# Attention of a hybrid layer: values as weights and the shares of two to four heads as the moving side, shares divided before they are stored, and gates transposed early

## The reference, cut to what matters

```
q_b = rms_norm(c_q @ a_wuq, a_qn_g);  k_b = rms_norm(bk, a_kn_g);  v_b = bv
score = sum_h relu(q_idx[h] @ k_idx.T) * w_idx[h]      # which keys each query may use
valid = top 64 of score, and key <= query
sc = where(valid, q_b @ k_b.T * 128 ** -0.5, -inf)
p = softmax(sc)                                        # exp(sc - max) / sum
y_b = (p @ v_b) * silu(bz)                             # bz: channels projected by w_in
out = x + concat(y_a, y_b, y_c) @ w_out
```

## Time and profile before

| what | value |
|---|---|
| median of three runs | 1543.57 us |
| the profiled execution | 1543.47 us |
| its span | 1541.8 us |
| TensorE busy | 1537.1 us |
| DVE, ACT, POOL busy | 992.7, 752.8, 337.6 us |
| granted clock of TensorE | 1.000 of full speed (2.4 GHz) over the span |

### The profile page before, as it was taken

The page is one execution under the profiler, slowest core; times in us unless marked ns, Lnnn a source line. Parts: engine busy times, 40 slices in busy tenths (PEclk is TensorE's granted clock), DMA queues, the critical chain, the costliest instruction groups (busy, mean ns, idle before and its releaser), DMA issues.

```text
span 1541.8 us, 18904 instructions
## 1 busy us (share of the span) xinstructions
PE 1537.1 (100%) x7048; PEld 1274.7 (83%) x7048; DVE 992.7 (64%) x1524; ACT 752.8 (49%) x1006; POOL 337.6 (22%) x575
## 2 busy tenths in 40 slices
PE   9999999999999999999999999999999999999999
PEld 7888888888888888888878888888888888888887
DVE  6647555667768864576579667675556776664554
ACT  5745444587544444554545545535346444443332
POOL 6041112230020040126420354345300120200000
PEclk9999999999999999999999999999999999999999
DMA  9886778886686685568856787898975776666684
GB/s 297 245 240 196 224 212 231 213 233 190 206 231 204 194 220 163 158 181 274 245 187 179 218 255 208 234 272 243 268 246 174 252 219 192 206 201 193 194 249 157
DMA packets 201673, 335.43 MB, mean 218 GB/s; under 512 B 48115, under 2 KB 56709, under 8 KB 201325
## 3 DMA queue, kind: packets, MB, share of 16 engines
q1 hardware_dynamic: 181468, 288.20, 62.5%
q0 software_dynamic: 20064, 46.00, 11.2%
q10 hardware_dynamic: 48, 0.02, 0.0%
HBM read 311.50 MB, written 22.44 MB: 217 GB/s over the span
## 4 chain that ended last, share of the span: by engine, by line
PE 98%; DVE 1%; ACT 1%; issue 0%; DMA 0%; DVEq 0%
PE acc L1006 31%; PE acc L1009 31%; PE acc L1008 31%; PE mix L1068 1%; PE mix L1148 1%; PE mix L977 1%; PE mix L1061 0%; PE mix L1137 0%; PE acc L1216 0%; DVE w_lo L1622 0%; ACT w_hi L1286 0%; PE mix L1134 0%; PE mix L1124 0%; PE mix L1122 0%; DMA xs<-in_x_dram 0%
## 5 line engine op out<-in xcount | busy, mean ns | idle before, releaser
L1622 DVE TENSOR_TENSOR w_lo<-w_raw,w_hi 128x1024 fp32r<-128x1024 f32 (+2 forms) x535 | 647.1, 1220 | 421.2 <-ACT w_hi L1286 417.8
L1286 ACT ACTIVATE w_hi<-w_raw 128x1024 fp32r<-128x1024 f32 (+2 forms) x535 | 556.5, 1050 | 525.2 <-PE acc L1009 460.0
L1006 PE MATMUL acc<-w_hi,op_hi 128*128 128x512 f32 (+1 forms) x2036 | 799.8, 393 | 0.3 <-DVE w_lo L1622 0.3
L1009 PE MATMUL acc<-w_hi,op_lo 128*128 128x512 f32 (+1 forms) x2036 | 792.9, 389 | 0.0
L1008 PE MATMUL acc<-w_lo,op_hi 128*128 128x512 f32 (+1 forms) x2036 | 791.9, 389 | 0.0
L1009 PEld LDWEIGHTS acc<-w_hi,op_lo 128*128 128x128 f32 x2036 | 382.2, 188 | 80.1
L1006 PEld LDWEIGHTS acc<-w_hi,op_hi 128*128 128x128 f32 x2036 | 382.5, 188 | 79.5 <-issue 1.3
L1008 PEld LDWEIGHTS acc<-w_lo,op_hi 128*128 128x128 f32 x2036 | 382.5, 188 | 77.7
L762 POOL DMA_DIRECT2D conv_dram<-y x48 | 30.8, 696 | 171.2 <-ACT y L1338 170.4
L762 POOL DMA_DIRECT2D y_dram<-y x32 | 20.5, 708 | 184.8 <-DVE y L2052 115.0
L904 POOL DMA_DIRECT2D bp_dram<-b_ps x48 | 31.4, 713 | 71.3 <-ACT b_ps L1506 66.6
(11 more groups left out here) (339 smaller groups left out, 963.3 us busy)
## 6 DMA issues: line engine op xcount, KB each, us to landing
w_raw<-in_w_in_dram SPq DMA_DIRECT2D x367, 512.0 KB, 4.6
w_raw<-in_w_out_dram SPq DMA_DIRECT2D x128, 512.0 KB, 4.5
w_raw<-in_w_in_dram SPq DMA_DIRECT2D x16, 384.0 KB, 3.3
w_raw<-in_a_wuq_dram SPq DMA_DIRECT2D x12, 512.0 KB, 5.7
conv_dram<-y POOLq DMA_DIRECT2D x48, 64.0 KB, 3.8
y<-conv_dram POOLq DMA_DIRECT2D x48, 64.0 KB, 4.8
w_raw<-in_a_wuqi_dram SPq DMA_DIRECT2D x6, 512.0 KB, 4.6
bp_dram<-b_ps POOLq DMA_DIRECT2D x48, 64.0 KB, 4.2
```

Of the source, the lines that this page charges most:

```text
L1006: nc.tensor.matmul(o, hi[:, kt, tok], hv[:, i, n0:n1], start=(kt == (kts if late else blk["kts"])[0]), stop=False)
L1009: last_mm = nc.tensor.matmul(o, lo[:, kt, tok], hv[:, i, n0:n1], start=False, stop=(kt == blk["kts"][-1]))
L1286: func(split_ap(w_hi, c), w_raw[:, c % RAW_BUFS, 0:n], ACT.Copy).then_inc(hi_ready, 1)
L1622: vec.tensor_tensor(split_ap(w_lo, c), w_raw[:, c % RAW_BUFS, 0:n], split_ap(w_hi, c).bitcast(F32), ALU.subtract).then_inc(lo_ready, 1)
```

## The change

- **The product with the values.** In `bo` the values of one key block are now the stationary side, and the shares of all heads of the part are the moving side: one matmul of 512 columns in part 0, two of 256 columns in parts 1 and 2, where the two key blocks are summed. The result has channels on the partitions and tokens along the row.
- **The division.** DVE multiplies the exponentials by the reciprocal in place, 128x512, right behind the reciprocal in piece `bs`, and signals `b_scaled`. POOL stores the shares after `b_scaled`, no longer after `b_exp`. In `bo` DVE only multiplies by the gate, in one instruction a part.
- **The gates.** Since the result has channels on the partitions, the gate has to be turned before it. SP now stores and brings back the 512 gate channels of a group right after they have been projected: `y_keep` waits for the evacuation of that block, and stands 10 chunks behind it, `y_bring` 14. The two `yd` of a group are written 14 and 14 to 19 chunks behind the block's end, those of the last group 34 and 35. ACT's `yt` of these channels waits for the last `bo` of the group.

```diff
@@ plan
+    for g, slots in enumerate(((14, 19), (14, 17), (14, 18), (34, 35))):
+        for i, slot in enumerate(slots):
+            weave(end("silu", W_A + 512 * g) + slot, [("yd", 4 + 2 * g + i)])
...
-        weave(at + (18, 18, 18, 14)[g], [("yd", 4 + 2 * g), ("yd", 5 + 2 * g)], 4)
@@ sync, y_keep
-                wait_read(sp, "bo", (g, 2))
+                wait_stored(sp, "silu", W_A + 512 * g)
...
-                    if name == "bo" and arg[1] == 2:
-                        y_ready[c + RAW_BUFS + AHEAD + 3] = arg[0]
+                    if name == "evac" and blocks[arg]["kind"] == "silu" and blocks[arg]["arg"] < W_A + W_B:
+                        y_ready[c + RAW_BUFS + AHEAD + 3] = (blocks[arg]["arg"] - W_A) // 512
@@ gpsimd, keep_shares
-                pool.wait_ge(b_exp, n + 1)
+                pool.wait_ge(b_scaled, n + 1)
@@ tensor, bo
-                for i in range(4):
-                    val = kv[:, 0 if v == 0 else i % 2, 512 + g * P:512 + g * P + P]
-                    o = i if v == 0 else i // 2
-                    ins = nc.tensor.matmul(bank(use)[:, o * P:o * P + P], b_pT[:, (3 * g + v) % 2, i, :], val,
-                                           start=(v == 0 or i % 2 == 0), stop=(v == 0 or i % 2 == 1))
+                shares = b_pT[:, (3 * g + v) % 2]
+                val = [kv[:, m, 512 + g * P:512 + g * P + P] for m in range(M)]
+                if v == 0:
+                    ins = nc.tensor.matmul(bank(use)[:], val[0], shares.rearrange("p a t -> p (a t)"), start=True,
+                                           stop=True)
+                else:
+                    for m in range(M):
+                        ins = nc.tensor.matmul(bank(use)[:, 0:SEQ], val[m],
+                                               shares.rearrange("p (a m) t -> p m a t", m=M)[:, m], start=(m == 0),
+                                               stop=(m == 1))
@@ scalar, yt
+                if 4 <= i < 12:
+                    wait_read(act, "bo", ((i - 4) // 2, 2))
@@ vector, bs
                 step(vec.reciprocal(b_scale(v)[:, 0:n], b_scale(v)[:, 0:n]))
+                p3 = b_ps[:, (3 * g + v) % 2].rearrange("p (h k) -> p h k", h=n)
+                vec.tensor_tensor(p3, p3, b_scale(v)[:, 0:n].unsqueeze(2).to_broadcast([P, n, w]),
+                                  ALU.mult).then_inc(b_scaled, 1)
@@ vector, bo
-                for i in range(4 if v == 0 else 2):
-                    ...
-                    ins = vec.scalar_tensor_tensor(dst, bank(use)[:, i * P:i * P + P], b_scale(v)[:, i:i + 1], dst,
-                                                   ALU.mult, ALU.mult)
+                dve.wait_ge(y_turned, yd_order.index(5 + 2 * g) + 1)
+                part = y[:, :, W_A + 512 * g:W_A + 512 * g + 512].rearrange("p q (j t) -> p q j t", j=2)
+                ...
+                ins = vec.tensor_tensor(dst, src, dst, ALU.mult)
```

More of the change, by code:

```diff
@@ L436, in hybrid_kernel @@
         b_exp = sem("b_exp")
+        b_scaled = sem("b_scaled")
         a_one = sem("a_one")
@@ L2004, in bo @@
                 g, v = arg
-                m = 0 if v == 0 else 1
+                dve.wait_ge(y_turned, yd_order.index(5 + 2 * g) + 1)
+                part = y[:, :, W_A + 512 * g:W_A + 512 * g + 512].rearrange("p q (j t) -> p q j t", j=2)
                 wait_filled(dve, use)
-                for i in range(4 if v == 0 else 2):
-                    h = 4 * g + (i if v == 0 else 2 * v - 2 + i)
-                    dst = y[:, m, W_A + h * P:W_A + h * P + P]
-                    ins = vec.scalar_tensor_tensor(dst, bank(use)[:, i * P:i * P + P], b_scale(v)[:, i:i + 1], dst,
-                                                   ALU.mult, ALU.mult)
+                if v == 0:
+                    dst = part[:, :, :, 0:P]
+                    src = bank(use)[:].rearrange("p (q j t) -> p q j t", q=2, j=2)
+                else:
+                    dst = part[:, v - 1, :, P:SEQ]
+                    src = bank(use)[:, 0:SEQ].rearrange("p (j t) -> p j t", j=2)
+                ins = vec.tensor_tensor(dst, src, dst, ALU.mult)
                 done_bank(ins, use)
```

## The result

| | before | after |
|---|---|---|
| median of 6 runs | 1543.75 us | 1550.70 us |
| lowest to highest | 1542.53 to 1544.80 | 1548.08 to 1552.68 |
| profiled execution, span | 1543.47, 1541.8 | 1550.93, 1549.2 |

What follows compares the result with a forecast made beforehand. TensorE, busy 1537.1 of 1541.8 us, was taken as the bound. The profiled 1543.47 us less 0.4 us for the product, all else priced 0, gave 1543.1, as a median 1543.2 us; range 1542.2 to 1546.3 us.

Steps and rivals of the forecast that it cites:

- Part 4: Gates' transfers on SP: removing old places wins nothing; new ones behind chunks 217, 233, 249, 265 cost about 0.
- rival A: Weights late at the gates' new places behind chunk 233, 249 or 265: 1543.9 to 1546.8 us; chance 0.28.
- Groups 0 and 1: Gates stored behind chunks 217 and 233: 0 for the first; 0, or up to 0.5 us, for the second.
- the sign: If right, ACT waits some microseconds for weights behind each new `y_keep`, around 680, 722, 765 us, none at 1120.
- Group 2: Gates stored behind chunk 249: lead full, 5.6 us against a load 5.0 us late; price 0.
- The old place: Former gate transfers: ACT waited 6.65 us for chunk 387's weights, TensorE did not stand; removal wins nothing.
- The product: Swapped sides in `bo` on TensorE: fewer records, 0.24 us plus 0.18 us, in sum 0.4 us less.
- the lower bound of my pair: Part 0's 512-column matmul in `bo`: gain no better than the 256-column piece, 0.03 us; upper bound 0.06 us.
- D: Gap in the moving side of `bo`, parts 1 and 2, halves the reading rate: 7 us, 1550 us; chance 0.03.
- DVE and shares: DVE some 5 us more work, division hidden in a 0.86 us gap; shares stored 0.7 us later; price 0 each.
- B: Shares come back late, DVE waits in `bpt` and weights queue behind: 3 us, 1546 us; chance 0.06.
- C: A freer DVE also shrinks TensorE's waits, at most 0.3 us beside the 0.4: 1542.9 us; chance 0.06.

Runs made afterwards that it cites:

- The early transposes: Changed kernel with DVE's transposes of the first index queries one chunk earlier, ahead of `w_lo` of chunk 270: 1544.38 us against 1543.43 for the kernel before.
- the last version: Changed kernel with gates of group 2 stored behind chunk 275, group 3 behind 287, ways back four chunks on: 1542.90 us against 1543.33 for the kernel before.
- the small transfers: Changed kernel, last gates' way back behind chunk 277, eight transfers with an eighth of the bytes at its former place: 1548.47 us against 1543.22 before.

## Why the prediction was wrong, point by point

- **The failed step** is in Part 4 and in rival A: "behind chunk 265 (group 3): chunk 266 has a lead ... About 0 is left." For chunk 266 the result was near: TensorE waited 0.4 us. But I read a late load only by the lead of that chunk's own matmuls. Each `w_lo` is also a place in DVE's queue, and whatever is written behind it inherits its delay, with a room of its own. Behind `w_lo` of chunk 270 that room was 2.2 us (0.24 us in which DVE stood idle ahead of the transposes, and 2.0 us until L1122). This `w_lo` was 7.4 us late, and TensorE, itself 0.7 us later by then, stood 4.4 us at the index scores. The early transposes show it: same `w_lo`, no wait.
- **Chunk 270 was not looked at.** I weighed the first load behind each store. The way back four chunks later meets POOL's transfers of index queries, and a load already late by the buffer chain from 266. The landing time of 8.9 us against 5.5 was in no term. A's own count for the way back put chunk 266 up to 6.5 us late, not chunk 270; TensorE did stand for lateness at the new places, but for the queries behind it.
- **SP's time for the store** was taken as 6.41 us, with the pack ending at about 758.5 us. It took 8.06 us and ended at 762.34 us. That is 3.8 us later, for two reasons. The store itself was 1.65 us longer; why, no run shows. The busy share of the DMA engines, 1.02 in this stretch, is that of the old place (1.01) and doesn't explain it:

```profile
754.00:762.00 8.00, 8.00 (x36) 6.44 (x35) 4.90 (x6) 3.73 (x5) 5.10 (x8) 1.00 1.02 222
```

  The other reason is that the pack also began late. The load of chunk 265 ahead of it was issued at 753.87 us in after and at 752.01 us before. In the last version, where group 2's pack is moved away, it is at 752.01 us again. So the lateness left by group 2's pack reached group 3's, and the forecast priced each place by itself.
- **The clock** was not in the sum: a single wait of 4.4 us costs 2.6 us more through the half clock. Rival A's upper end of 3.6 us was worked out without it, so even A's own path was bounded too low.
- **Groups 0 and 1** passed as forecast for TensorE. ACT did not even wait for weights behind the store of group 1, where the sign named a wait around 680 us; behind those of groups 2 and 3 it waited, 4.74 us at 722 and 6.55 us at 767 us. Group 2 was called full (5.6 us against 5.0): in nine executions of that stretch it cost 0 to 1.6 us, by the same chain over DVE's `b_kT`. That step was too sure. The profiled execution of after has 0 there. The 5.6 us is read rightly (chunk 250 before: 727.48 - 721.90 us), but it is not "three chunks less the 1.23 us", which would be 3 x 2.72 - 1.23 = 6.9; ACT's 1.06 us come ahead of DVE's.
- **The old place**: I expected no wait of ACT on weights at 1120 us. ACT indeed waits for TensorE there, and 3.0 us for weights once more, at 1127 us, which I did not follow; TensorE loses nothing, so the removal won nothing, as said.
- **The product**: 12 parts at 1.32 us across, from 1.36, are 0.4 to 0.5 us, as forecast. The 512-column piece is no better than two of 256, the lower bound of my pair. The gap in the moving side costs nothing that these rows show. D falls.
- **DVE and shares**: 12 divisions of 692 ns, DVE busy 3.6 us more (forecast 5), hidden in the gap named; no wait for shares. DVE's waits for the queries `b_qT` grew from 1.2 to 3.5 us, with no wait of TensorE behind them. B falls. C got nothing.

Not settled: why the place at chunk 258 varies from execution to execution, as one profile each doesn't tell it; and why the store of group 3 holds SP longer than the others.

## What to carry to other kernels

When a transfer or a load is made late, don't read only the slack of its own user: list what stands behind it in each engine's queue until the lateness is absorbed, and take the smallest room among them. Do the same one round of buffers later, since a late buffer delays its next load. And look at the clock behind a wait of TensorE: here one of 4.4 us cost 2.6 us more, one of 2.0 us cost nothing more.

## What the runs showed of the hardware

- After standing 4.4 us TensorE was granted 0.50 for the stretch up to 788.0 us, 5.7 us; after standing 0.9 us, behind 18 matmuls, it stayed at 1.00. After standing 2.0 us (the small transfers) it kept full speed too: mean clock over the span 1.000.
- Eight ways back held SP 3.83 us with 8 KB and 3.84 us with 64 KB each; eight stores of 64 KB held it 5.5 us at 665 us and 8.1 us at 754 us in after, and 6.4 to 6.8 us at the four old places.
- Loads of 512 KB took 5.5 us to land before and 8.9 us after (medians) in the same stretch (768 to 774 us), in which the changed kernel also moves its ways back.
